# Head sums of squares of two chunks in four 64x64 quarters of TensorE, and the first of them placed one projection group later

## The reference, cut to what matters

```python
def l2_norm(x):
    return x * lax.rsqrt(jnp.sum(x * x, axis=-1, keepdims=True) + EPS)
...
qkv = jax.nn.silu(causal_depthwise_conv(jnp.concatenate([q, k, v], axis=-1), conv_w))
...
qh = l2_norm(heads(q)) * HEAD_DIM ** -0.5
kh = l2_norm(heads(k))
...
qa = rms_norm(dq.reshape(B, T, DSA_HEADS, HEAD_DIM), dsa_q_norm[l])
ka = rms_norm(dk.reshape(B, T, DSA_HEADS, HEAD_DIM), dsa_k_norm[l])
```

## Time and profile before

| | |
|---|---|
| median of three runs | 2151.27 us |
| lowest and highest | 2148.92, 2152.72 us |
| the profiled execution's own time | 2148.25 us |
| its span, first to last instruction | 2146.4 us |
| TensorE (PE) busy | 2123.1 us, 99% |
| VectorE (DVE) busy | 1044.4 us, 49% |
| ScalarE (ACT) busy | 758.5 us, 35% |
| GpSimd (POOL) busy | 353.0 us, 16% |

### The profile page before, as it was taken

How to read it: one execution, slowest core, us unless ns; L and a number is a source line. 1 busy time by engine, 2 the same in 40 slices (tenths; PEclk the granted TensorE clock), 3 DMA queues, 4 the chain that set the end, 5 groups by cost and what they waited for, 6 DMA issues and landing times.

```text
span 2146.4 us, 31599 instructions
## 1 busy us (share of the span) xinstructions
PE 2123.1 (99%) x13057; PEld 1718.4 (80%) x13057; DVE 1044.4 (49%) x1419; ACT 758.5 (35%) x1046; POOL 353.0 (16%) x293
## 2 busy tenths in 40 slices
PE   9999999999999999999999999999999999999999
PEld 7888888777777888888888888887777778888887
DVE  5343333688666643433333433337886655433322
ACT  5222222474445422222232222234743454222211
POOL 0111011105013411101111010111040135010000
PEclk9999999999999999999999999999999999999999
DMA  5222223221111232222222222232212102222232
GB/s 195 98 93 91 100 94 110 103 99 42 60 52 39 79 117 91 92 89 105 94 98 98 98 98 91 94 129 94 85 42 91 41 20 101 96 96 98 93 108 74
DMA packets 30643, 192.38 MB, mean 90 GB/s; under 512 B 3216, under 2 KB 5392, under 8 KB 11984
## 3 DMA queue, kind: packets, MB, share of 16 engines
q1 hardware_dynamic: 30160, 189.80, 24.9%
q10 hardware_dynamic: 384, 1.14, 0.1%
HBM read 188.70 MB, written 2.10 MB: 89 GB/s over the span
## 4 chain that ended last, share of the span: by engine, by line
PE 89%; DVE 6%; ACT 2%; issue 1%; DMA 0%; SPq 0%; POOL 0%; DVEq 0%; ACTq 0%
PE psum L895 27%; PE psum L897 26%; PE psum L896 26%; PE psum L1326 2%; PE psum L1026 1%; PE psum L1310 1%; DVE wl L1749 1%; PE psum L1198 1%; PE psum L1195 1%; DVE acc L1832 1%; PE psum L1294 1%; DVE XL L1764 1%; DVE gkT L1863 0%; DVE wrk L1847 0%; PE psum L1268 0%
## 5 line engine op out<-in xcount | busy, mean ns | idle before, releaser
L895 PE MATMUL psum<-XH,wh 128*128 128x512 f32 x1904 | 760.4, 399 | 3.8 <-DVE wl L1749 1.8
L897 PE MATMUL psum<-XH,wl 128*128 128x512 f32 x1904 | 742.4, 390 | 0.0
L896 PE MATMUL psum<-XL,wh 128*128 128x512 f32 x1904 | 742.2, 390 | 0.0
L895 PEld LDWEIGHTS psum<-XH,wh 128*128 128x128 f32 x1904 | 357.9, 188 | 91.8 <-issue 14.4
L897 PEld LDWEIGHTS psum<-XH,wl 128*128 128x128 f32 x1904 | 357.8, 188 | 75.7
L896 PEld LDWEIGHTS psum<-XL,wh 128*128 128x128 f32 x1904 | 358.1, 188 | 74.3 <-issue 4.3
L1757 DVE TENSOR_TENSOR wl<-raw,wh 128x2048 fp32r<-128x2048 f32 x88 | 201.7, 2292 | 159.4 <-ACT wh L1396 159.4
L895 PE MATMUL psum<-HH,wh 128*128 128x512 f32 x704 | 273.9, 389 | 0.0
L896 PE MATMUL psum<-HL,wh 128*128 128x512 f32 x704 | 273.9, 389 | 0.0
L897 PE MATMUL psum<-HH,wl 128*128 128x512 f32 x704 | 273.9, 389 | 0.0
L1391 ACT ACTIVATE wh<-raw 128x2048 fp32r<-128x2048 f32 (+1 forms) x84 | 157.2, 1872 | 301.1 <-PE psum L897 301.1
(11 more groups left out here) (250 smaller groups left out, 1970.3 us busy)
## 6 DMA issues: line engine op xcount, KB each, us to landing
raw<-weights SPq DMA_DIRECT2D x143, 1024.0 KB, 4.8
raw<-weights SPq DMA_DIRECT2D x32, 896.0 KB, 4.4
xT<-xt SPq DMA_DIRECT2D x4, 512.0 KB, 6.2
memT<-memt SPq DMA_DIRECT2D x2, 1024.0 KB, 4.9
out<-xT SPq DMA_DIRECT2D x8, 256.0 KB, 5.8
stripsA<-strip_table SPq DMA_DIRECT2D x2, 768.0 KB, 6.3
raw<-weights SPq DMA_DIRECT2D x2, 512.0 KB, 6.5
stripsB<-strip_table SPq DMA_DIRECT2D x2, 512.0 KB, 7.4
```

Of the source, the lines that this page charges most:

```text
L895: pe.matmul(out_ap, a_hi, b_hi, start=first, stop=False)
L896: pe.matmul(out_ap, a_hi, b_lo, start=False, stop=False)
L897: return pe.matmul(out_ap, a_lo, b_hi, start=False, stop=last)
```

## The change

Three edits that belong together:

1. The sums of two chunks, nj even and nj odd, are made together when the odd one is due. Four matmuls with a 64x64 block of ones each take one 64-row half of one nsq buffer and write one 64-row half of one bank: chunk 0 to bank 2 in place, chunk 1 to bank 3 with the halves swapped. Two 128x128 matmuls over both chunks become four 64x64 ones.
2. rs of the odd chunk undoes the swap: Ln is done in two instructions of 64 partitions each, then one Exp. rs and ap of the even chunk move to the step of the odd one.
3. In `_order`, silu_qk, sq 0 and sq 1 go from behind conv 7 to behind conv 8. hs, rs and ap 0 and 1 go from behind mm gz0 to behind mm gz1; those of 2 and 3 from behind mm gz1 to behind mm gz2, ahead of ev gz2; sq 2 and 3, and sq 4 and 5, move along.

```diff
-            ["silu_qk"], []]
+            [], ["silu_qk"]]
...
-        if n == 7:
+        if n == 8:
             norm("sq", *pairs(0))
 
     def factors(i):
-        for kind in ("hs", "rs", "ap"):
+        norm("hs", pairs(i)[1])
+        for kind in ("rs", "ap"):
             norm(kind, *pairs(i))
 
     mm("gz", 0)
-    factors(0)
     ev("gz", 0)
-    norm("sq", *pairs(1))
     put(("idx", 4))
     sel(1)
     mm("gz", 1)
-    factors(1)
+    factors(0)
     ev("gz", 1)
-    norm("sq", *pairs(2))
+    norm("sq", *pairs(1))
     put(("idx", 5))
     mm("gz", 2)
+    factors(1)
     ev("gz", 2)
+    norm("sq", *pairs(2))
     put("silu_vz")
...
-    later = [(1, ("sq", 8)), (2, ("hs", 8)), (2, ("rs", 8)), (3, ("ap", 8))]
+    later = [(1, ("sq", 8))]
...
-                    later.extend([(0, ("sq", nj)), (2, ("hs", nj)), (2, ("rs", nj)), (3, ("ap", nj))])
+                    later.append((0, ("sq", nj)))
+                    if nj % 2:
+                        later.extend([(2, ("hs", nj)), (2, ("rs", nj - 1)), (2, ("rs", nj)),
+                                      (3, ("ap", nj - 1)), (3, ("ap", nj))])
...
                         pe.wait_ge(S["nq_sq"], nj + 1)
-                        if nj == 0:
+                        if nj == 1:
                             pe.wait_ge(S["row_ready"], 1)
-                        if nj == 8:
+                        else:
+                            pe.wait_ge(S["nq_r"], nj - 1)
+                        if nj == 9:
                             pe.wait_ge(S["v_done"], NB)
-                        if nj >= 2:
-                            pe.wait_ge(S["nq_r"], nj - 1)
-                        pe.matmul(bank[2 + nj % 2][:, 0:n], const("same64"), nsq[nj % 2][:, 0:n],
-                                  start=True, stop=True).then_inc(S["nq_ss"], 1)
+                        for i in range(2):
+                            for par in range(2):
+                                mm = pe.matmul(bank[2 + i][rows[par ^ i], 0:n], const("ones")[rows[par], 0:DH],
+                                               nsq[i][rows[par], 0:n], start=True, stop=True)
+                            mm.then_inc(S["nq_ss"], 1)
...
-                        rsqrt(nrr[nj % 2][:, 0:n], bank[2 + nj % 2][:, 0:n], 1.0 / DH if name in ("mk", "dk") else 1.0,
-                              const("eps64") if name in ("dq", "mq") else None).then_inc(S["nq_r"], 1)
+                        scale = 1.0 / DH if name in ("mk", "dk") else 1.0
+                        bias = const("eps64") if name in ("dq", "mq") else eps
+                        if nj % 2 == 0:
+                            rsqrt(nrr[0][:, 0:n], bank[2][:, 0:n], scale, bias).then_inc(S["nq_r"], 1)
+                            return
+                        for par in range(2):
+                            chain.step(act.activation(nrr[1][rows[par], 0:n], bank[3][rows[1 - par], 0:n], ACT.Ln,
+                                                      bias=bias[rows[par], :], scale=scale))
+                        chain.join()
+                        act.activation(nrr[1][:, 0:n], nrr[1][:, 0:n], ACT.Exp, scale=-0.5).then_inc(S["nq_r"], 1)
```

## The result

| | kernel before | changed kernel |
|---|---|---|
| median, lowest, highest | 2151.99, 2148.29, 2155.95 us | 2165.18, 2159.36, 2170.76 us |
| ratio, 95% interval | | 1.0063, 1.0048 to 1.0078 |
| profiled execution, its span | 2148.25, 2146.4 us | 2164.17, 2162.4 us |
| mean granted clock of the profiled execution | 0.999 | 0.994 |
| TensorE busy | 2123.1 us | 2125.6 us |

The change costs 13 us; the forecast was +4.6 (2155.9), and 2165.18 lies above its range, which ended at 2161. Slower was right, the size was not. (Of the eight executions before, one was disturbed: the median counts it, the highest time leaves it out.)

A forecast was written before the change was run, and what follows sets the result against it. TensorE, 99% busy, was taken as the bound, its saving subject to ScalarE's and VectorE's queues. Per layer 4.4 later up to mq0, 3.1 saved behind it and 1.0 of new waits gave +2.3, +4.6 for two: 2155.9 us, range 2149.5 to 2161.

The forecast's parts named there:

- What bounds the kernel: Whole span: TensorE is 99% busy, so work taken out saves its time unless the next instruction waits for another engine.
- Part 1, the quarters: All sums: four 64x64 matmuls run at once, 0.96 us a pair, saving 5.0 us of TensorE work a layer.
- the extra 0.07 a pair: Sums 8 to 15: each pair behind 64x64 pieces costs some 0.07 us more than one full sum, 0.3 in all.
- rival C: Pairs of sums: quarters go two at a time, each late pair 0.86 us dearer; 2163 to 2166 us, 5%.
- Part 2, the walk: First sums up to mq0: queues walked with old durations; waits of 1.9, 1.0 and 2.1 us, layer 4.4 us later.
- Part 3, behind mq0: Behind mq0 in each layer: sums 8 to 15 give back 3.1 us, new waits cost 1.0.
- wait for the copy NN: Behind mq0: with sum 10 gone, the ScalarE copy has 0.86 us less cover; 0.5 estimated.
- that for the state: At sums 14 and 15: two ap steps on VectorE ahead of the state St make TensorE wait 0.66 us more.
- The sum: Whole kernel: 4.4 - 3.1 + 1.0 = +2.3 us a layer, +4.6 for two, 2155.9 us.
- rival D: Near the new waits: granted clock falls, 1.4 us a stretch, in one or both layers 2157.3 to 2158.7 us; 15%.
- A: Up to mq0: the new waits do not form and the saved passes arrive, 11.4 us faster, 2139.9 us; 10%.
- B: Queues move faster than walked, or nothing new behind mq0: 0 to +1.9 us a layer, 2151 to 2155; 20%.

The follow-up runs named there:

- copy_first: Changed kernel with the copy of gz2 put ahead of rs and ap of chunks 2 and 3; 2164.5 us, ratio 1.0059 to the kernel before.
- before_two_idles: Kernel before with two idle TensorE waits added a layer, 1.6 us at mk1 and 1.9 at mq0; 2161.6 us, ratio 1.0049.
- before_idle: Kernel before with TensorE also waiting idle ahead of mq0 for the copy of mv1, about 1.9 us a layer; 2158.6 us, ratio 1.0037.
- fill: Changed kernel with 21 useless matmuls a layer in the waits ahead of mk1, mv0 and sums 6 and 7; 2159.5 us, ratio 1.0036.

## Why the prediction missed

- **What bounds the kernel.** Right as far as it went: TensorE's saving is worth something only where it does not wait, and up to mq0 it waits.
- **Part 1, the quarters.** Four at once, as argued: 0.86 a pair at 512 columns where 0.96 was taken. From the last piece ahead of a pair to the second matmul behind it are 1.345 us, and 1.341 for one single sum before: the extra 0.07 a pair was nothing. By the bank rule of the Trainium skill ("TensorEngine Tiling (Array Packing)", Gotcha 1: PSUM Pressure) different row tiles cannot access one bank at the same time. Two quarters at a time would be 1.7 us a pair, an estimate from that rule and the 0.86. The two halves of one bank are written by two row halves of the array here, and the measurement decides: 0.86, so rival C is out. That its price, 2163 to 2166, holds the measured 2165.2 is chance.
- **Part 2, the walk.** Right. In the old trace's times mk0 was to end at 469.8 and ended at 469.7; the waits were forecast 1.9, 1.0 and 2.1 and came as 1.9, 1.0 (second layer) and 2.1 or 2.5; mq0 was forecast 4.4 later and came 4.9 later in the first layer, 5.4 in the second, with some 0.5 of low clock in the latter. One term is said too small in words: idx 5 "about 1.1 late", where the walk's own times put gz2 at 460.2, 2.2 late. It started at 460.0, 2.0 late, and the 4.4 was added up from the times, so it is right.
- **Part 3, behind mq0.** Forecast -3.1 + 1.0 = -2.1 a layer. Measured, low clock taken out: 1.4 - 3.4 = -2.0 and 2.3 - 4.4 = -2.1. The wait for the copy NN grew from 0.2 to 0.9 a layer, 0.7 more (estimate 0.5), that for the state by 0.65 (0.66).
- **The sum.** +4.6 for what it counted; rest rose by 3.1. The forecast had 2155.9 with a range to 2161, and 2165.2 came: the sum has no term for the granted clock.
- **What failed is rival D,** the price of the low clock that the waits bring: nothing in the sum, and too little in the rival. It was written as an accident beside the forecast: 15%, one stretch in a layer at 1.4 us, "in one or both layers 2157.3 to 2158.7", with the range's upper end at 2161. The runs show 1.7 us a stretch (the earlier trace rows end at 625, and the stretch goes on to 625.7) and on average six more of them in an execution, 10.2 us. The prediction had seen that "waits of 1.9 and 1.0 us, 2.8 us apart, are close to that pattern", and left out the third, 2.1 us, which it forecast itself for the same 16 us. It also took the low clock as either there or not, from a single profiled execution that had one stretch, while the runs shown, 2148.9 to 2152.7, already differed by steps of that size: the kernel before loses 4.9 us to it on average. The rule "sum of the waits" needs a second term, and here it was three times the first.
- That A was unlikely was right for the reason given, the two full queues; copy_first shows that the wait at mk1 is theirs. Of B neither part came: the queues were as slow as walked and the part behind mq0 had its new waits. That the rest of 3.1 lies in B's 0 to 3.8 is likely an effect of the split into rest and low clock, which makes the rest too small.

## What to carry to other kernels

Work taken off TensorE where another engine sets the pace becomes idle time, and several waits close together cost from half as much (before_two_idles: 3.4 us for 6.9 of waits) to about as much again (the changed kernel: 10.2 us for some 11 us of waits up to mq0) in granted clock: price new waits with the clock behind them, and look at the clock of several executions, not of one. Change the form of a step first only where the engine that it relieves is the bound (here behind mq0, 6 us gained), and leave the order alone where the others are. A wait can be tested in a few lines by putting useless matmuls into it: if the kernel gets faster, the clock was the cost. If it does not, as with the single wait of before_idle, nothing is settled.

## What the runs showed of the hardware

- A low stretch need not follow a wait at once. In fill, where TensorE stands still for at most 0.4 us at a time between 460 and 499, the clock falls behind six matmuls of only six rows (they fill 2.84 us), and the third stretch of the changed kernel, at 498, has the same place. The same matmuls at 487.11 in the trace of before are followed by full clock. Timeline of TensorE in fill:

```profile
492.57 2.84 PE L1151 MATMUL psum<-rowg,cst 6*128 6x512 f32 x6
495.33 0.80 PE L899 MATMUL psum<-XH,wh 128*128 128x512 f32 x1
495.92 0.63 PE L900 MATMUL psum<-XL,wh 128*128 128x512 f32 x1
```

 Why the clock falls there in one and not in the other was not tried, and it stands against a cause that is idle time alone.
- Executions of one kernel differ in how much low clock they have: the changed kernel's eight run from 2159.4 us at a clock of 0.995 to 2170.8 at 0.991, 11.4 us for 0.004 of 2165 (8.7), so the clock explains most of the spread.
- Low clock cost little in a place where TensorE is not the bound: in the changed kernel's first layer the stretch at 474 takes the place of the wait of 1.0 at mv0, which only the second layer has, and mq0 comes no later for it (+4.9 us against +5.4).
